# The merge levels of the delta stage as 32x32 tiles

## The reference

```
def step(S, inp):
    qc, kc, vc, gc, bc = inp
    decay = jnp.exp(jnp.where(incl, gc[..., :, None] - gc[..., None, :], -jnp.inf))
    kbeta = kc * bc[..., None]
    a = jnp.where(strict, jnp.einsum('bhid,bhjd->bhij', kbeta, kc) * decay, 0.0) + eye
    rhs = jnp.concatenate([vc * bc[..., None], kbeta * jnp.exp(gc)[..., None]], axis=-1)
    sol = lax.linalg.triangular_solve(a, rhs, left_side=True, lower=True, unit_diagonal=True)
    u, w = sol[..., :DV], sol[..., DV:]
    v_new = u - jnp.einsum('bhck,bhkv->bhcv', w, S)
    attn = jnp.einsum('bhid,bhjd->bhij', qc, kc) * decay
    o = (jnp.einsum('bhck,bhkv->bhcv', qc * jnp.exp(gc)[..., None], S)
         + jnp.einsum('bhij,bhjv->bhiv', attn, v_new))
    ...
```

## Time and profile before

| | us |
|---|---|
| median of three runs | 4460.0 (4459.9 to 4460.61) |
| profiled execution | 4463.48 |
| its span, first to last instruction | 4461.9 |
| TensorE busy in the span | 4206.4 (94%) |
| VectorE, ScalarE, POOL busy | 2111.2, 1620.5, 901.9 |
| mean granted TensorE clock | 0.972 of full speed |

### The profile page before, as it was taken

One profiled execution on the slowest core, in us unless ns is written; L12 is line 12 of the kernel. 1 busy time (PEld: TensorE's weight loads), 2 busy tenths in 40 slices (PEclk: granted clock), 3 DMA queues, 4 the chain that ended last, 5 costly groups with the idle time before them and its releaser, 6 DMA issues. The chain is left out here.

```text
span 4461.9 us, 84521 instructions
## 1 busy us (share of the span) xinstructions
PE 4206.4 (94%) x33615; PEld 4021.3 (90%) x33615; DVE 2111.2 (47%) x2850; ACT 1620.5 (36%) x2858; POOL 901.9 (20%) x655
## 2 busy tenths in 40 slices
PE   7999998998999999899897889999999999999993
PEld 6999997887989999899885688999999999999993
DVE  4556665765431111333335544444454455545554
ACT  5863332555210000222115434534344444444442
POOL 2434211433433323243211222000000000000001
PEclk9999999999999999999999999999999999999996
DMA  3223687565422222343100125556565666666675
GB/s 92 78 83 93 177 220 197 143 172 159 127 79 89 83 87 79 114 123 104 51 19 4 30 88 145 160 156 168 164 176 166 183 174 187 174 188 186 183 209 201
DMA packets 999025, 592.76 MB, mean 133 GB/s; under 512 B 114961, under 2 KB 957298, under 8 KB 998818
## 3 DMA queue, kind: packets, MB, share of 16 engines
q1 hardware_dynamic: 924112, 511.18, 41.2%
q10 hardware_dynamic: 65970, 52.44, 3.9%
q0 software_dynamic: 8736, 26.26, 1.8%
HBM read 493.67 MB, written 95.72 MB: 132 GB/s over the span
## 5 line engine op out<-in xcount | busy, mean ns | idle before, releaser
L2662 DVE TENSOR_TENSOR experts_w<-experts_raw,experts_w 128x1024 fp32r<-128x1024 f32 x352 | 415.6, 1221 | 144.4 <-ACT experts_w L2626 144.4
L210 PE MATMUL experts_pa<-experts_hx,experts_w 128*128 128x264 f32 (+6 forms) x1408 | 411.9, 293 | 2.9 <-DVE experts_w L2662 2.9
L210 PE MATMUL experts_pd<-experts_hid,experts_w 128*128 128x264 f32 (+6 forms) x1408 | 410.4, 291 | 0.0
L212 PE MATMUL experts_pa<-experts_hx,experts_w 128*128 128x264 f32 (+6 forms) x1408 | 409.3, 291 | 0.0
L210 PE MATMUL experts_pb<-experts_hx,experts_w 128*128 128x264 f32 (+6 forms) x1408 | 409.0, 291 | 0.0
L211 PE MATMUL experts_pa<-experts_hx,experts_w 128*128 128x264 f32 (+6 forms) x1408 | 409.0, 290 | 0.0
L211 PE MATMUL experts_pd<-experts_hid,experts_w 128*128 128x264 f32 (+6 forms) x1408 | 408.8, 290 | 0.0
L212 PE MATMUL experts_pd<-experts_hid,experts_w 128*128 128x264 f32 (+6 forms) x1408 | 408.5, 290 | 0.0
L212 PE MATMUL experts_pb<-experts_hx,experts_w 128*128 128x264 f32 (+6 forms) x1408 | 408.4, 290 | 0.0
L211 PE MATMUL experts_pb<-experts_hx,experts_w 128*128 128x264 f32 (+6 forms) x1408 | 407.9, 290 | 0.0
L210 PE MATMUL proj_pm<-hT,proj_w_hi 128*128 128x384 f32 (+1 forms) x1152 | 388.1, 337 | 0.3 <-POOL proj_w_lo L671 0.3
(11 more groups left out here) (439 smaller groups left out, 10661.9 us busy)
## 6 DMA issues: line engine op xcount, KB each, us to landing
experts_raw<-in_moe_w SPq DMA_DIRECT2D x352, 512.0 KB, 4.7
experts_raw<-in_moe_w SPq DMA_DIRECT2D x128, 704.0 KB, 5.9
projected<-proj_out SPq DMA_DIRECT2D x48, 544.0 KB, 3.8
proj_w<-in_gdn_w_in ACTq DMA_DIRECT2D x48, 512.0 KB, 4.2
ffnup_w<-in_ffn_w SPq DMA_DIRECT2D x44, 512.0 KB, 5.1
ffndown_w<-in_ffn_w SPq DMA_DIRECT2D x32, 704.0 KB, 4.7
mixout_w<-in_gdn_w_out SPq DMA_DIRECT2D x32, 512.0 KB, 4.2
hidden<-ffnup_hid ACTq DMA_DIRECT2D x22, 544.0 KB, 2.7
```

The costliest lines, as they stand in the source:

```text
L210: pe.matmul(out, as_r(w_hi), as_r(x_hi), start=first, stop=False)
L212: return pe.matmul(out, as_r(w_lo), as_r(x_hi), start=False, stop=last)
L2662: dve.tensor_tensor(as_r(w[:, u, 1, x, 0:KD, :]), raw[:, x, u, 0:KD, :], w[:, u, 0, x, 0:KD, :], ALU.subtract).then_inc(split[x][u], 1)
```

## The change

The constants get two columns, one for each side of a pair of 32-row quarters, with -1 in the partitions of its own quarters and 0 in the others. The products x and d are done in tiles of 32x32: `quarter(q)` is one of four groups of 32 partitions, `own_cols(q)` the columns of its block in the 64 of its head. At the first level x does the four diagonal tiles; d does two tiles for the one form of T and four for the other. At the second level x does the two tiles below the diagonal, and d two. `X` and the copy of ScalarE shrink to 32 columns a pair. VectorE's subtraction becomes multiply-adds on 128 elements a partition: three at the first level, one at the second; the factor takes only the partitions whose quarter the columns belong to. Nothing else in the stage's order changes.

```
-CONST_W = RAMP + 33
+R_SIDE = 33
+CONST_W = RAMP + 35
...
+    for side in range(2):
+        tail[:, R_SIDE + side] = -1.0 * (np.arange(P) // (2 * SUB) % 2 == side)
...
-        X = each("X", [P, PAIRS, CHUNK])
+        X = each("X", [P, PAIRS, 2 * SUB])
...
+        Q = 2 * SUB
+        quarter = lambda q: slice(Q * q, Q * q + Q)
+        own_cols = lambda q: slice(Q * (q % 2), Q * (q % 2) + Q)
+        minus = lambda side: m["const"][:, RAMP + R_SIDE + side:RAMP + R_SIDE + side + 1]
...
-                    for i, hp in both:
-                        last = pe.matmul(b_x[ch][rows(hp), 0, i, :], BT[rows(hp), slot, l, PAIRS * ch + i, :], TT[rows(hp), slot, 0, PAIRS * ch + i, :], start=True, stop=True)
+                    for i in range(PAIRS):
+                        p = PAIRS * ch + i
+                        if l == 0:
+                            for q in range(4):
+                                last = pe.matmul(b_x[ch][quarter(q), 0, i, 0:Q], BT[quarter(q), slot, l, p, own_cols(q)], TT[quarter(q), slot, 0, p, own_cols(q)], start=True, stop=True)
+                        else:
+                            for q in (0, 2):
+                                last = pe.matmul(b_x[ch][quarter(q + 1), 0, i, 0:Q], BT[quarter(q), slot, l, p, own_cols(q + 1)], TT[quarter(q), slot, 0, p, own_cols(q)], start=True, stop=True)
...
-                        if l < L - 1:
-                            for hp in range(2):
-                                pe.matmul(b_x[ch][rows(hp), 0, i, :], TT[rows(hp), slot, 1, PAIRS * ch + i, :], X[ch][rows(hp), i, :], start=True, stop=True)
-                        for hp in range(2):
-                            last = pe.matmul(b_x[ch][rows(hp), 1, i, :], X[ch][rows(hp), i, :], TT[rows(hp), slot, 1, PAIRS * ch + i, :], start=True, stop=True)
+                        p = PAIRS * ch + i
+                        if l == 0:
+                            for q in (0, 2):
+                                pe.matmul(b_x[ch][quarter(q), 0, i, 0:Q], TT[quarter(q), slot, 1, p, own_cols(q)], X[ch][quarter(q), i, :], start=True, stop=True)
+                            for q in range(4):
+                                last = pe.matmul(b_x[ch][quarter(q), 1, i, 0:Q], X[ch][quarter(q), i, :], TT[quarter(q), slot, 1, p, own_cols(q)], start=True, stop=True)
+                        else:
+                            for q in (1, 3):
+                                last = pe.matmul(b_x[ch][quarter(q - 1), 1, i, 0:Q], X[ch][quarter(q), i, :], TT[quarter(q), slot, 1, p, own_cols(q)], start=True, stop=True)
...
-                    act.activation(X[ch][:, :, :], b_x[ch][:, 0, :, :], ACT.Copy).then_inc(e["x_copied"], 1)
+                    act.activation(X[ch][:, :, :], b_x[ch][:, 0, :, 0:Q], ACT.Copy).then_inc(e["x_copied"], 1)
...
-                    which = slice(0, 2) if l < L - 1 else slice(1, 2)
...
-                    now = TT[:, slot, which, pairs(ch), :]
-                    dve.tensor_tensor(now, now, b_x[ch][:, which, :, :], ALU.subtract).then_inc(e["t_new"], 1)
+                    if l == 0:
+                        for way, side in ((0, 0), (1, 0), (1, 1)):
+                            now = TT[:, slot, way, pairs(ch), own_cols(side)]
+                            last = dve.scalar_tensor_tensor(out=now, in0=b_x[ch][:, way, :, 0:Q], scalar=minus(side), in1=now, op0=ALU.mult, op1=ALU.add)
+                    else:
+                        now = TT[:, slot, 1, pairs(ch), own_cols(1)]
+                        last = dve.scalar_tensor_tensor(out=now, in0=b_x[ch][:, 1, :, 0:Q], scalar=minus(0), in1=now, op0=ALU.mult, op1=ALU.add)
+                    last.then_inc(e["t_new"], 1)
```

More of the change, by code:

```diff
@@ L88, in constants @@
         x[X_LVL + n] = -1.0 * ((cj // (2 * s) == ci // (2 * s)) & (cj % (2 * s) < s) & (ci % (2 * s) >= s))
-    tail = np.zeros((P, 33), np.float32)
+    tail = np.zeros((P, 35), np.float32)
     tail[:, R_DESC:R_DESC + NE] = NE - np.arange(NE)
```

## The result

The change made the kernel slower: 4470.66 us in the median of 13 runs against 4460.0 of the kernel before, ratio 1.0022 with an interval of 1.0015 to 1.003. The forecast was 4442, faster. The profiled execution took 4471.79 us.

The account below looks back on a forecast made before the run. TensorE was taken to bound the delta stage; eight quiet passes at -1.57 us and eight with a solve at -0.7 gave -18 us, hence 4442 us. The range of 8 in 10 was 4434 to 4484.

Parts of the forecast that it names:

- x0: First-level x: 64 records on four tiles, 0.48 us against 0.93, but only 0.05 gained, since d0 waits for copy X.
- d0: First-level d: 96 records instead of 64, 0.96 us against 1.92, before 0.10 lost to a change of tile shape.
- R1: TensorE step between d0 and x1; the new change of tile shape from it to x1 was to lose 0.10 us.
- x1: Second-level x: 32 records, half as wide, on two tiles, 0.48 us against 0.93, so 0.45 saved a pass.
- d1: Second-level d: 32 records, half as wide, 0.45 us saved at most, less 0.10 for a change of tile shape.
- End of the pass: TensorE's turns with VectorE behind its last products: of the 0.35 us from d1, 0.31 could be taken.
- Passes with a solve: Eight of 16 passes, where VectorE also solves rows and its updates start later: 0.7 us saved in each.
- The rivals on the record's price: TensorE's records keep today's 30 ns pace: 4495 us, chance 0.30; or are handed over at 17 to 22 ns: 4451 to 4469, 0.20.
- the fast side: A 32x32 record costs 30 ns divided by the tiles sharing the stream: 4432 to 4451 us, chance 0.50.
- The wait for VectorE: Rival: x1 waits for VectorE's third update in every pass, 4449 us; counted within the 0.50 of the fast side.
- ScalarE, POOL, the queues: Other engines and transfers: nothing added or moved but two constant columns at the kernel's start, no wait; at nothing.
- a fall of the clock: In the delta stage, clock below 1.00 because smaller tiles leave more of the array unused; no size or chance given.

Follow-up runs that it names:

- e6: e1 with each product of x1 and d1 issued twice into the same place, 64 records more in a pass: 4481.19 us, ratio 1.0044 to the kernel before.
- e1: The kernel before with only the second level's x1 and d1 in 32x32 tiles, no record added: 4452.23 us, ratio 0.9981.
- e8: e1 with d0's upright products also in 32x32 tiles, issued ahead of the others, no record added: 4451.89 us, ratio 0.9982 to the kernel before.

## Why the prediction was wrong

**x0.** Forecast 0.05, measured 0.35: from x0's start to d0's it was 935.53 - 933.43 = 2.10 and is 927.28 - 925.53 = 1.75. The copy X did not hold d0 back in this pass. **d0** 1.92 to 1.13 with its change of shape, a gain of 0.79; forecast 0.86. **R1** to x1 0.14 longer, forecast 0.10. **x1** 1.02 to 0.62 and **d1** 0.98 to 0.62, so 0.40 and 0.36; forecast 0.45 before any change of shape for the one, 0.35 with it for the other. **End of the pass**, R3 to R0: 5.03 to 5.25, 0.22 lost where 0.04 was forecast. Together -1.54; forecast -1.57. That the two sums meet so closely is luck: the 0.30 more at x0 is made up by the end of the pass (0.18 less) and by smaller misses at d0, R1 and x1. And this is the best pass; two others without a long stall took 17.09 and 17.32. Passes with a solve and no long stall take 17.43 to 18.21 us, 0.2 to 1.0 less than 18.44; forecast 0.7.

**The rivals on the record's price** are settled for the fast side. x0's 64 records end their starts within 0.75 - 0.19 = 0.56 us, 9 ns each; the 0.19 is the view's length of a single such record. x1's additional 32 records in e6 took 1.20 - 0.69 = 0.51 us, 16 ns each on two tiles. The Trainium skill's rule that starts never come closer than about 25 ns ("TensorE: Matmul & The Clock Gate", section on the 56 ns gap) does not hold for these streams: its estimate of +1.1 us a pass stands against a measured -1.54. The wait for VectorE comes to 2.5 us, 1.2 of them before the first pass and the rest in solving passes.

**The step that failed** is "ScalarE, POOL, the queues: no transfer is added or moved but two more columns of the constants ... At nothing." Transfers were added, of instructions: 128 more records a pass are half a block more, and x0, T and d0, 4.02 us of issuing before (933.43 to 937.45), shrank to 2.88 (925.53 to 928.41) with 336 records in it instead of 208. The forecast priced each record on the array and took it for granted that the records were there; the stalls end only 2.5 to 2.8 us after a packet of them starts. With the undisturbed passes the stretch would be 296.93 - 8 x 1.54 - 8 x 0.6 = some 280 us; it was 308.78. Idle by issue inside it is 22.8 us (0.9 before), 21.9 of the 29; the other 7 are what is left over. The lower clock behind the stalls (0.95 on the mean, 1.00 in the earlier trace rows) has a part in them: R1, x1 and R2 took 995.50 - 987.18 = 8.32 us behind the stall at 986.72, 932.91 - 928.41 = 4.50 in the quiet pass. How the 7 divide is not shown. The profiled execution took only 8.3 us more than the one before, so what lies outside the stretch took 3.5 less; why is not shown either.

The prediction also named a fall of the clock as what could break it, for a reason that the trace does not bear out: the clock was 1.00 through small tiles where no stall stood, as in the window of the densest stretch, and was below it during and behind the longest stalls.

**What beats both kernels**, by 0.2%, is the second level alone: e1 at 0.9981 and e8 at 0.9982, with no record added.

## What to carry to other kernels

Smaller tiles of the array cost by what they stream and run side by side, but each is an instruction, and an engine's instructions are transfers too: before splitting products, count how many records will stand in the densest two or three microseconds, and what loads run then. Where the count must not rise, take the part of the change that adds none. Idle time "by issue" inside a loop of products that wait for nothing, at whole numbers of blocks from one another, is the sign to look for.

## What the hardware showed that was not expected

- Stalls of 1 to 5 us at the seams of blocks of 251 to 252 records of TensorE (2265, 3272, 1508 and 1511 records between them), in kernels whose shortest stretch of 256 records takes 2.3 to 3.6 us; none over 1.8 us where it takes 4.2 or more.
- One 16 KB instruction packet for each block (52 for 13041 records); the seven stalls in the table end 2.5 to 2.8 us after one starts.
- In the 3.5 to 4.3 us behind three of the longer stalls the granted clock was 0.50 to 0.69, and R1 took 3.68 us instead of 1.96, so that such a stall costs more than its own length; behind one of 1.03 us it stayed at 1.00.
- A stream of 32x32 records on four tiles starts one every 9 ns, on two tiles one every 16 ns; entering or leaving the shape costs about 0.10 us each time, and two chains that alternate pay it twice.
- An increment of a semaphore on TensorE takes 0.15 us in its order.
